# Expert results stored under their entry's row, in a 4 MB buffer that the routing fills completely

## The reference, cut to what matters

```python
expert_id = grp * EXPERTS_PER_GROUP + top_i        # [512, 2]
A = N * EXPERT_TOPK                                # 1024 entries: (token, first or second choice)
...
hid = jax.nn.silu(xblk @ w_gate[e]) * (xblk @ w_up[e])
yb  = hid @ w_down[e]                              # one row per entry
...
y = segment_sum(yb * buf_w[:, None], buf_tok)      # each token: weight * row, over its two entries
h = h + gt2 * y ;  out = rmsnorm(h, norm_final_g)
```

## Time and profile before

| | |
|---|---|
| median of 3 runs | 1327.46 us |
| the profiled execution: time, span | 1324.34 us, 1322.7 us |
| mean granted TensorE clock | 0.921 |
| busy: PE, DVE, ACT, POOL | 84%, 29%, 17%, 13% |
| DMA: total, on SP's queue, on POOL's queue | 311.42 MB, 273.82 MB, 32.32 MB |

### The profile page before, as it was taken

One profiled execution on the slowest core, in us unless ns is written; L12 is line 12 of the kernel. 1 busy time (PEld: TensorE's weight loads), 2 busy tenths in 40 slices (PEclk: granted clock), 3 DMA queues, 4 the chain that ended last, 5 costly groups with the idle time before them and its releaser, 6 DMA issues. The chain is left out here.

```text
span 1322.7 us, 16833 instructions
## 1 busy us (share of the span) xinstructions
PE 1117.6 (84%) x7205; PEld 579.5 (44%) x7205; DVE 388.7 (29%) x645; ACT 219.0 (17%) x443; POOL 173.9 (13%) x220
## 2 busy tenths in 40 slices
PE   6999999599997887999889993988887878867870
PEld 5543444344465555888745451333323333323330
DVE  3334527322004454345522335110011001010004
ACT  4011224020003453333300120000000000000002
POOL 2100002024001343304100001001000000000003
PEclk8899999679998998898999995989989989899995
DMA  9512639934225000000072628899999999999965
GB/s 363 193 64 95 223 120 344 405 147 135 96 95 136 2 1 25 3 2 4 3 280 82 263 77 315 362 428 426 426 427 427 428 427 424 427 428 427 425 263 200
DMA packets 60741, 311.42 MB, mean 235 GB/s; under 512 B 8772, under 2 KB 15270, under 8 KB 47098
## 3 DMA queue, kind: packets, MB, share of 16 engines
q1 hardware_dynamic: 47210, 273.82, 51.7%
q0 software_dynamic: 11152, 32.32, 6.5%
q10 hardware_dynamic: 2304, 4.20, 0.8%
HBM read 284.62 MB, written 33.04 MB: 240 GB/s over the span
## 5 line engine op out<-in xcount | busy, mean ns | idle before, releaser
L2361 PE MATMUL ps<-ring,zrT 128*64 128x512 f32 x704 | 163.3, 618 | 29.8 <-issue 26.9
L899 PE MATMUL ps<-ring,uT 128*128 128x512 f32 x384 | 169.8, 599 | 1.2 <-PE ps L899 0.6
L2381 PE MATMUL ps<-ring,hdT 128*64 128x512 f32 x352 | 121.7, 634 | 11.5 <-issue 9.5
L890 PE MATMUL ps<-uT,ring 128*128 128x512 f32 x256 | 114.2, 603 | 2.1 <-DVE uT L623 1.4
L899 PEld LDWEIGHTS ps<-ring,uT 128*128 128x128 f32 x384 | 72.4, 192 | 93.1 <-issue 93.1
L2361 PEld LDWEIGHTS ps<-ring,zrT 128*64 128x64 f32 x704 | 56.5, 142 | 127.5 <-issue 126.9
L2169 DVE TENSOR_TENSOR zrT<-zrT,ps 128x512 f32<-128x512 f32 x16 | 11.0, 687 | 284.1 <-PE ps L2361 284.1
L2361 PE MATMUL ps<-mg,zrT 128*64 128x512 f32 x160 | 75.7, 629 | 8.1 <-issue 8.1
L1976 ACT ACTIVATE zrT<-ps 128x512 f32<-128x512 f32 x16 | 9.6, 597 | 413.0 <-PE ps L2361 413.0
L890 PEld LDWEIGHTS ps<-uT,ring 128*128 128x128 f32 x256 | 48.5, 192 | 67.0 <-issue 65.9
L1897 POOL DMA_INDIRECT y_dram<-zrT,y_at x16 | 16.2, 1012 | 437.5 <-DVE zrT L2178 437.5
(11 more groups left out here) (385 smaller groups left out, 1484.3 us busy)
## 6 DMA issues: line engine op xcount, KB each, us to landing
ring<-in_moe_w_gate_dram SPq DMA_DIRECT2D x22, 2048.0 KB, 30.1
ring<-in_moe_w_up_dram SPq DMA_DIRECT2D x22, 2048.0 KB, 32.6
ring<-in_moe_w_down_dram SPq DMA_DIRECT2D x22, 2048.0 KB, 33.5
ring<-in_w_in_dram SPq DMA_DIRECT2D x8, 2048.0 KB, 14.6
ring<-in_w_ada_dram SPq DMA_DIRECT2D x8, 2048.0 KB, 10.1
y_dram<-vrep POOLq DMA_DIRECT2D x1, 15872.0 KB, 59.0
mod<-in_moe_w_up_dram SPq DMA_DIRECT2D x5, 2048.0 KB
mg<-in_moe_w_up_dram SPq DMA_DIRECT2D x5, 2048.0 KB, 30.7
```

Source lines behind the costliest of these rows:

```text
L890: ins = pe.matmul(ps[:, n % 4, :], slot(name, KD, w)[:, k, c0:c0 + P], uT[:, k, :], start=(k == 0), stop=(k == KD - 1))
L899: ins = pe.matmul(ps[:, n % 4, :], uT[:, k, P * i:P * i + P], w, start=(k == 0), stop=(k == KD - 1))
L2361: ins = pe.matmul(ps[HALF * r:HALF * r + HALF, "gu".index(kind), :], xgT[:, b % 2, k, HALF * r:HALF * r + HALF], w[r][:, k, :], start=(k = ...
L2381: ins = pe.matmul(ps[HALF * r:HALF * r + HALF, 2 + c, :], hdT[:, j, HALF * r:HALF * r + HALF], w[r][:, j, 512 * c:512 * c + 512], start=(j ...
```

## The change

Each entry, choice j of token t, gets row 512 j + t of a buffer of 1024 rows. The table of destination rows comes from a second set of 8 matmuls over the same one-hot matrices, with a factor `entry_down` (8 minus the number of the entry's tile) in place of the token's tile; empty places again get a row out of bounds. Expert blocks, further ones too, store by that table. As every row is written exactly once, the clearing DMA and its wait go. In the end the 8 tiles lie in order in memory, and SP loads them with plain DMAs, behind a wait for all stores and behind `further`, to which a last wait is added for the case of overfull blocks. SP's first load into slot 8 also waits for the second set of matmuls.

```diff
     parts["tile_down"] = np.broadcast_to(NT - np.tile(np.arange(NT), 2), (P, 2 * NT))
-    parts["y_row"] = i[:, None] + P * np.arange(NPAIR)[None, :]
+    parts["entry_down"] = np.broadcast_to(2 * NT - np.arange(2 * NT), (P, 2 * NT))
...
-        y_dram = nc.dram_tensor("y_dram", [NBLK * P, D], F32).ap()
+        y_dram = nc.dram_tensor("y_dram", [2 * T, D], F32).ap()
...
             sem(f"c_{n}") for n in "ld pe kc blk g1 th h kT dve v0".split())
...
                     pool.tensor_tensor(bt[:, c, :], av[:, :], eis[c % 2][:, :], ALU.mult).then_inc(w_b, 1)
-                    if c == 0:
-                        pool.wait_ge(c_v0, 2)
-                        pool.dma_start(y_dram.rearrange("(p b) (a d) -> p (b a) d", p=P, a=2),
-                                       vrep[:, :].unsqueeze(1).to_broadcast([P, 2 * NBLK, 512]))\
-                            .then_inc(c_fill, 16)
...
                         dve.wait_ge(c_v0, 2)
-                        dve.wait_ge(c_fill, 16)
                         link(dve.scalar_tensor_tensor(h3, h2, 1.0, hx, ALU.add, ALU.mult))
...
-        row_y = alloc(top, "row_y", [P, NT, 2], I32)
...
-        y_at = alloc(top, "y_at", [P, NPAIR], I32)
...
+        y_at = alloc(top, "y_at", [P, NBLK], I32)
...
         at_block = rb("at_block", [P, 2 * NT, 2, NBLK], BF16)
+        at_entry = rb("at_entry", [P, 2 * NT, NBLK], BF16)
         hi = rb("hi", [P, NBLK])
...
             sem(f"e_{n}") for n in "xT xe g sl u hd hT he d y".split())
...
-        x_clear, r_ya = sem("x_clear"), sem("r_ya")
-        y_rows = y_dram.rearrange("(b p) d -> b p d", p=P)
+        x_clear, r_ya, r_ent = sem("x_clear"), sem("r_ya"), sem("r_ent")
+        y_rows = y_dram.rearrange("(j i p) d -> i j p d", j=2, p=P)
...
                 elif turns == 0 and s_ == 8:
-                    eng.wait_ge(r_tab, 1)
+                    eng.wait_ge(r_ent, 1)
                     eng.wait_ge(r_ov, 1)
...
-        def further(eng, first, body):
+        def further(eng, first, body, last=None):
...
                     body(v)
+                if last is not None:
+                    last()
...
-                further(sp, first, body)
+                def last():
+                    sp.wait_ge(v_st, 16 * OVER)
+
+                for q_ in range(2):
+                    sp.wait_ge(y_st[q_], 16 * (NPAIR // 2))
+                further(sp, first, body, last)
+                for i in range(NT):
+                    for j in range(2):
+                        sp.dma_start(ya[2 * i + j], y_rows[i, j]).then_inc(f_in[2 * i + j], 16)
                 sp.wait_ge(m_wr, 80)
...
                     pool.indirect_dma_start(y_dram, bass.IndirectOffsetOnAxis(ap=y_at[:, b:b + 1], axis=0), yo[:, b % 2, :],
-                                            None, bounds_check=NBLK * P - 1, oob_is_err=False)\
+                                            None, bounds_check=2 * T - 1, oob_is_err=False)\
                         .then_inc(y_st[b % 2], 16)
...
                     pool.tensor_copy(idx[:, 0:1], slots[:, bass.ds(v + NPAIR, 1)]).then_inc(v_idx, 1)
+                    pool.tensor_copy(idx[:, 1:2], y_at[:, bass.ds(v + NPAIR, 1)]).then_inc(v_row, 1)
                     pool.wait_ge(v_idx, v + 1)
+                    pool.sem_inc(v_seen, 1)
+                    pool.wait_ge(v_row, v + 1)
                     pool.sem_inc(v_seen, 1)
...
                     pool.wait_ge(v_y, 2 * v + 2)
-                    pool.dma_start(y_rows[v + NPAIR], yo[:, 0, :]).then_inc(v_st, 16)
+                    pool.sem_inc(v_seen, 1)
+                    pool.indirect_dma_start(y_dram, bass.IndirectOffsetOnAxis(ap=idx[:, 1:2], axis=0), yo[:, 0, :],
+                                            None, bounds_check=2 * T - 1, oob_is_err=False).then_inc(v_st, 16)
                     pool.wait_ge(v_st, 16 * v + 16)
...
                 further(pool, first, body)
-                pool.wait_ge(r_row, 1)
-                for i in range(NT):
-                    for j in range(2):
-                        n = 2 * i + j
-                        pool.indirect_dma_start(ya[n], None, y_dram,
-                                                bass.IndirectOffsetOnAxis(ap=row_y[:, i, j:j + 1], axis=0))\
-                            .then_inc(f_in[n], 16)
-                for n in range(2 * NT):
-                    pool.wait_ge(f_in[n], 16)
...
                    ALU.mult).then_inc(r_at, 1)
-                link(dve.scalar_tensor_tensor(R_, B_, float(P), X_, ALU.mult, ALU.add))
-                dve.tensor_copy(row_y[:, :, :].rearrange("p i j -> p j i"), R_).then_inc(r_row, 1)
+                TT(at_entry[:, :, :], oh_blk[:, :, :], C("entry_down").unsqueeze(2).to_broadcast([P, 2 * NT, NBLK]),
+                   ALU.mult).then_inc(r_row, 1)
                 dve.wait_ge(r_tab, 1)
...
                 dve.tensor_tensor(slots[:, :], hi[:, :], ps[:, 2, 0:NBLK], ALU.add).then_inc(r_sl, 1)
-                link(TS(yfar[:, :], hi[:, 0:NPAIR], float(T), float(NBLK * P), ALU.is_ge, ALU.mult))
-                dve.tensor_tensor(y_at[:, :], yfar[:, :], C("y_row"), ALU.add).then_inc(r_ya, 1)
+                dve.wait_ge(r_ent, 1)
+                link(TS(hi2[:, :], ps[:, 3, 0:NBLK], -float(P), 2.0 * T, ALU.mult, ALU.add))
+                dve.tensor_tensor(y_at[:, :], hi2[:, :], ps[:, 2, 0:NBLK], ALU.add).then_inc(r_ya, 1)
...
                 ins.then_inc(r_tab, 1)
+                pe.wait_ge(r_row, 1)
+                for n in range(2 * NT):
+                    ins = pe.matmul(ps[:, 3, 0:NBLK], at_place[:, n, :], at_entry[:, n, :], start=(n == 0),
+                                    stop=(n == 2 * NT - 1))
+                ins.then_inc(r_ent, 1)
```

More of the change, by code:

```diff
@@ L325, in build @@
             sem(f"c_{n}") for n in "ld pe kc blk g1 th h kT dve v0".split())
-        c_fill = sem("c_fill")
         s_gd = [sem(f"s_gd{n}") for n in range(2)]
@@ L1673, in build @@
         over = alloc(top, "over", [1, 16], I32)
-        idx = alloc(top, "idx", [P, 1], I32)
-        y_at = alloc(top, "y_at", [P, NPAIR], I32)
+        idx = alloc(top, "idx", [P, 2], I32)
+        y_at = alloc(top, "y_at", [P, NBLK], I32)
         gf = mod[:, 0, :]
@@ L1731, in build @@
         at_block = rb("at_block", [P, 2 * NT, 2, NBLK], BF16)
+        at_entry = rb("at_entry", [P, 2 * NT, NBLK], BF16)
         hi = rb("hi", [P, NBLK])
-        yfar = rb("yfar", [P, NPAIR])
+        hi2 = rb("hi2", [P, NBLK])
         in0 = rb("in0", [1, OVER, E])
@@ L1752, in build @@
             sem(f"e_{n}") for n in "xT xe g sl u hd hT he d y".split())
-        v_ld, v_idx, v_x, v_xT, v_xe, v_g, v_sl, v_hd, v_hT, v_he, v_d, v_y, v_st, v_seen = (
-            sem(f"v_{n}") for n in "ld idx x xT xe g sl hd hT he d y st seen".split())
+        v_ld, v_idx, v_row, v_x, v_xT, v_xe, v_g, v_sl, v_hd, v_hT, v_he, v_d, v_y, v_st, v_seen = (
+            sem(f"v_{n}") for n in "ld idx row x xT xe g sl hd hT he d y st seen".split())
         gu = [A[f"moe_w_{n}"][0].rearrange("e (p k) n -> e p k n", k=KD) for n in ("gate", "up")]
```

## The result

The changed kernel takes 1312.8 us, the median of 4 runs (1309.92 to 1314.8), against 1328.45 us for the kernel before in runs on the same chip: a ratio of 0.9883 [0.9854, 0.9911]. The forecast was 1310.6 us, in a range of 1304.5 to 1316. Twice more, with other kernels beside it, the same text gave 0.9889 [0.9874, 0.9904] and 0.9874 [0.9855, 0.9892].

What follows compares the result with a forecast made beforehand. Transfers were taken to bound PE's stall, the weight stream the expert stage, and a series of waits the end. 13.6 + 0 + 0 + 3.3 = 16.9 us off 1327.46 gave 1310.6 us, range 1304.5 to 1316.

Steps and rivals of the forecast that it cites:

- The clearing: PE's stall at 250 to 266 us: without the clearing, ada11 lands sooner and the wait shrinks 15.66 to 2.1, gaining 13.6 us.
- late anyway: At PE's stall: ada11 and the gate unit behind it fight each other, so only the end gains; 1324.2 us, chance 0.05.
- The clock: PE's clock behind the stall: the shorter gap changes nothing, taken as 0; bounds 6.2 us saved, 6.8 us lost.
- the first rival: Behind PE's stall: the clock comes back sooner, up to 6.2 us more gain, 1304.4 us; chance 0.12.
- The router: Router's end: the second table delays slot 8's load by about 0.2 us, covered, cost 0; uncovered 0.2 to 0.6 us.
- both covers: Router's end: PE's 5.98 us idle before its first transposes and DMA engines empty from 826 to 830 us hide the delay.
- The stores: Expert stage: storing the same rows to scattered places instead of runs costs the weight stream 0.
- The fourth rival: Expert stage: scattered stores cost the stream, 16 times; at 1.5 us per store 1334.6 us; chance 0.03.
- The end: Behind the last store: plain SP loads start the sums 1.4 us sooner and save 1.9 us of waits, 3.3 us together.
- No DMA wait of DVE behind it: Sign at the end: after the first weighted sum DVE waits for no load, since gather waits of 2.3 us go.
- the 0.4 us for ACT: At the end: DVE reaches the first norming after 5.2 us but ACT's root takes 5.5, a new 0.4 us wait.
- the second rival: At the end: the loads share the engines and land together, so the end gains nothing; 1313.9 us, chance 0.10.

Runs made afterwards that it cites:

- half_clear: Changed kernel with a clearing DMA of half the size (7,680 KB) put back in the old place; 1313.93 us, ratio 0.9885 to the kernel before.
- after_again: The changed kernel timed and profiled once more, with nothing edited; 1314.9 us, ratio 0.9889 to the kernel before.
- double_clear: Changed kernel with two clearing DMAs of 15,872 KB, one behind the other, in the old place; 1326.68 us, ratio 0.9976 to the kernel before.
- late_clear: Kernel before with only its clearing DMA moved, issued at about 295 us rather than 204; 1330.98 us, ratio 1.0015.
- best: Changed kernel with ada11 in an earlier-free ring slot (exchanged with the first gate unit's) and SP passing `further` before its store waits; 1310.7 us, ratio 0.9859.
- clear_back: Changed kernel with the 15,872 KB clearing DMA back in its place, into a buffer nobody reads; 1327.94 us, ratio 0.9981 to the kernel before.
- table_x10: Changed kernel with the second table's 8 matmuls made ten times over, same result; 1314.75 us, ratio 0.988 to the kernel before.

## Why the prediction was right

**The clearing: right in mechanism and place, 13.6 forecast.** ada11 landed after 9.8 us (9.4 in half_clear) where 9.2 was taken, and PE waited 3.24 and 2.24 us where 2.1 was. PE went on 12.5 us sooner in the first pair of profiles, 13.6 in after_again, 13.1 in the averages of the table. The runs give 13.0 us (medians on one chip) to 14.5 us (means of all). The rival "late anyway" is refuted by half_clear and double_clear: the unit takes 22.3 us with the clearing beside it and 9.4 without, with the same gate unit behind it each time. That nothing behind the stall gives the gain back was also right, in this kernel; late_clear shows how near such a place lies.

**The clock: 0, right.** The low level went on as long after the short stall as after the long one: the first 16 matmuls of the next tile, in which it ends, took 8.60 us in after and 8.58 before. The row of before:

```profile
275.48 8.58 PE L899 MATMUL ps<-ring,uT 128*128 128x512 f32 x16
```

What the first rival wanted, up to 6.2 us, isn't there. The traces show more than the forecast's reason: the clock had come down before the stall began. It fell at about 241 us, while PE worked without a break through 32 matmuls of 24 columns, 9 us ahead of the gap. The stretches of before, columns window, length, busy us of PE, clock, DMA share, GB/s:

```profile
240.00:242.00 2.00, 2.00 (x15) 0.72 1.04 349
242.00:244.00 2.00, 2.00 (x11) 0.50 0.99 365
```

In best, with a gap of only 0.32 us, the clock is down from 242 us as well, and those 16 matmuls take 9.23 us. So the low level around the stall is not the stall's price, and shortening the stall gave none of it back.

What does scatter is the stretch behind it. From PE's going on to the first gather's issue it takes 547.7 us in the profile of before, 552.9 in after's, 549.0 and 549.3 in the two repeats; 553.1 in clear_back, 549.4 in half_clear. It goes with the execution and its clock, not with the change: between 394 and 480 us behind PE's going on the mean clock is 1.00 in the five profiles with the shortest such stretch, before among them, and 0.95 or 0.96 in after, clear_back and double_clear. These 5.2 us are most of why the first pair of profiles shows 9.5 us and the runs some 16. Another 0.8 us lies between the first gather and the restart of the stream (16.5 us before, 17.4 after), which scatters in the same way, from 16.4 us in double_clear to 17.7 in clear_back.

**The router: 0, right.** The table took 0.40 us. Slot 8's load came 2.47 us behind the first gather's issue, 2.21 before (815.81 against 813.60): 0.26 later, forecast 0.2. table_x10 shows both covers.

**The stores: 0, right.** 427 GB/s over 390 us, 10.4 us to landing where it was 10.5, and an expert stage of 461.5 us against 461.6. The fourth rival, over 1 us for each of 16 stores, would have shown there.

**The end: 3.3 forecast, 2.5 by the profiles, from partly wrong terms.** SP's step from the last store to the first load took 1.06 us where 1.8 was taken; the first load landed after 3.6 us, not 3.0, presumably as it shares the engines with the seven behind it. By luck the two errors cancel: the sum started 4.68 us behind the store, forecast 4.8. From DVE's first sum to the end of its last norming it took 16.68 us instead of 18.38, a gain of 1.7 where 1.9 was taken. "No DMA wait of DVE behind it" was wrong: the loads took a median of 6.6 and 7.3 us to land, and DVE waited for them 0.39 and 0.18 us in after; the 0.4 us for ACT that the forecast had in their place did not come. In after_again DVE waited 1.82 us, and the rows in its chain of waits and its timeline are:

```profile
1285.45 7.18 DMA uT<-y_dram
```
```profile
1292.65 1.28 DVE L2214 SCALAR_TENSOR_TENSOR h<-uT,wts,h 128x1024 f32<-128x1024 f32 x1 [1.82 <-DMA uT<-y_dram]
```

So the truth lies between the forecast and the second rival: over all profiles the end gives 2.5 us, counted from the last store's issue. That agrees with clear_back's 2.5 us [1.1, 3.9] in whole times, but the comparison without a clearing, 0.8 us with a standard error of 1.0, doesn't confirm it. In whole times the end's gain is not settled.

**The sum.** Forecast 16.9 us. The mean of all 12 runs of the changed kernel is 16.4 us under the mean of before, 1329.4 us: 13 to 14 from the clearing, some 2 to 3 from the rest.

## What to carry to other kernels

A large transfer with no urgency is paid for by the next urgent unit issued while it is in flight, so look for what is issued before it lands, and at what stands in the new place before you move it. To see how much the unit suffers, count both queues' packets in the window and compare their sizes. Of a wait that goes, ask what is late next, and look in the rows whether the clock was high before an idle gap of TensorE: in late_clear it was, and the gap cost slower matmuls behind it as well; in before it was down already. Where one profile of each kernel disagrees with the timed runs, find the stretch that scatters, and compare the rest between anchors on both sides of it.

## What the runs showed of the hardware

A 2 MB unit beside the clearing does not get half of the engines. ada11 moved 2.1 MB in 22.8 us, 92 GB/s of about 417; the compression weights 2.1 MB in 36.0 us, 58 GB/s. The DMA queues show the share: packets, MB and share of the engines' time, in before from 246 to 259 us, then in late_clear from 333 to 345 us. POOL's queue with the clearing is q0, SP's is q1; in late_clear a third queue, ACT's, moved another 0.52 MB in that time.

```profile
q0 software_dynamic: 885, 3.62, 67.7%
q1 hardware_dynamic: 890, 1.79, 35.4%
```
```profile
q0 software_dynamic: 866, 3.55, 71.7%
q1 hardware_dynamic: 866, 0.89, 20.7%
```

The two queues moved the same number of packets; but a packet of the clearing has 4.1 KB, one of ada11 2.0 KB and one of the compression weights 1.0 KB. So the clearing moved twice and four times their bytes. clear_back and double_clear show the same from 246 to 259 us, 887 packets of each, and 890 against 889. The Trainium skill, "DMA: Bandwidth & Descriptors", section "Queues, rings and completion order", has each engine take turns between the queues, a packet at a time; the even counts of these traces agree with that. No run varied the packet size of one and the same load. A second part of the 22.8 us is a late start: SP's queue moved no packet from 237 to 241 us and 38 from 241 to 243, where in after, from 2 to 4 us behind the issue, it moved 345. What delays them stays open.

The clearing of before, with the loads beside it, ran at 16.25 MB / 59.0 us = 275 GB/s.

An idle gap of 8.2 us of PE, with the clock at 1.00 before it, cost 16.2 us: the 64 matmuls behind it ran wholly at 1.2 GHz, and the next 48 began there. The gap of 15.66 us in before cost no more than its length: the clock was already down when it began, and came back as long behind the resumption as with the gap of 3.24 us.

Rows of 4 KB stored to scattered places cost the stream of 427 GB/s nothing that shows against rows in runs: 10.4 against 10.5 us to landing, 461.5 against 461.6 us for the expert stage.
